# A two-layer hybrid decoder trunk: spread of the condition, first norm, and the places of the adaLN sums

## What is computed

```python
cond = silu(c)
for l in range(2):
    sh1, sc1, g1, sh2, sc2, g2 = split(cond @ w_ada[l] + b_ada[l], 6)
    h = rms_norm(x, norm1[l]) * (1 + sc1) + sh1
    x = x + g1 * token_mixer(h, ...)   # three attention branches, gated, one output projection
    h = rms_norm(x, norm2[l]) * (1 + sc2) + sh2
    x = x + g2 * swiglu(h, w_gu[l], w_down[l])
```

## Time and profile before

| | |
|---|---|
| median of 3 runs | 1011.0 us (1010.39 to 1011.73) |
| profiled execution, its own time | 1010.04 us |
| its span, first to last instruction | 1008.2 us |
| TensorE busy | 934.6 us, 93% |
| VectorE busy | 695.9 us, 69% |
| ScalarE busy | 474.8 us, 47% |
| moved by DMA | 198.83 MB, mean 197 GB/s |
| mean granted TensorE clock | 0.964 |

### The profile page before, as it was taken

The page is one execution under the profiler, slowest core; times in us unless marked ns, Lnnn a source line. Parts: engine busy times, 40 slices in busy tenths (PEclk is TensorE's granted clock), DMA queues, the critical chain, the costliest instruction groups (busy, mean ns, idle before and its releaser), DMA issues.

```text
span 1008.2 us, 15872 instructions
## 1 busy us (share of the span) xinstructions
PE 934.6 (93%) x6716; PEld 885.0 (88%) x6716; DVE 695.9 (69%) x1097; ACT 474.8 (47%) x642; POOL 24.3 (2%) x48
## 2 busy tenths in 40 slices
PE   3899989999885999999988999899999989999998
PEld 2689979877884999999987899799779889999998
DVE  2977789786885778686845367897867754656443
ACT  4344976356232443443344349754553544434341
POOL 1000000000000000000000000000000000000000
PEclk9999999999895899999987999999999989999999
DMA  9777533414575488888852474334145525665541
GB/s 375 280 288 282 178 110 118 160 47 183 216 266 207 159 302 324 301 305 318 289 217 83 141 274 162 125 126 168 43 167 176 201 89 193 217 223 174 194 167 42
DMA packets 29446, 198.83 MB, mean 197 GB/s; under 512 B 3264, under 2 KB 3648, under 8 KB 7232
## 3 DMA queue, kind: packets, MB, share of 16 engines
q1 hardware_dynamic: 23184, 154.74, 43.1%
q0 software_dynamic: 5760, 41.95, 11.0%
q10 hardware_dynamic: 432, 1.14, 0.3%
HBM read 196.76 MB, written 1.05 MB: 196 GB/s over the span
## 4 chain that ended last, share of the span: by engine, by line
PE 67%; DVE 19%; ACT 9%; issue 3%; DMA 2%; ACTq 0%; DVEq 0%
PE bank L448 17%; PE bank L450 16%; PE bank L449 16%; DVE w_lo L1084 5%; ACT w_hi L819 3%; PE bank L526 3%; PE bank L527 3%; PE bank L528 3%; PE bank L470 2%; DVE front L1091 2%; DVE score L1246 2%; PE bank L545 2%; PE bank L544 2%; PE bank L546 2%; DVE acc L1337 1%
## 5 line engine op out<-in xcount | busy, mean ns | idle before, releaser
L1084 DVE TENSOR_TENSOR w_lo<-raw,w_hi 128x2048 fp32r<-128x2048 f32 (+2 forms) x146 | 314.2, 2160 | 138.8 <-ACT w_hi L819 138.6
L448 PE MATMUL bank<-h_hi,w_hi 128*128 128x256 f32 x1216 | 351.4, 289 | 9.1 <-DVE w_lo L1084 4.8
L819 ACT ACTIVATE w_hi<-raw 128x2048 fp32r<-128x2048 f32 (+2 forms) x146 | 262.7, 1806 | 185.0 <-PE bank L450 121.3
L449 PE MATMUL bank<-h_lo,w_hi 128*128 128x256 f32 x1216 | 347.6, 286 | 0.0
L450 PE MATMUL bank<-h_hi,w_lo 128*128 128x256 f32 x1216 | 347.5, 286 | 0.0
L448 PEld LDWEIGHTS bank<-h_hi,w_hi 128*128 128x128 f32 x1216 | 237.2, 195 | 13.1 <-issue 12.2
L449 PEld LDWEIGHTS bank<-h_lo,w_hi 128*128 128x128 f32 x1216 | 237.2, 195 | 0.1
L450 PEld LDWEIGHTS bank<-h_hi,w_lo 128*128 128x128 f32 x1216 | 236.9, 195 | 0.0
L448 PE MATMUL bank<-y_hi,w_hi 128*128 128x256 f32 x480 | 138.4, 288 | 5.5 <-DVE proj L1399 4.5
L449 PE MATMUL bank<-y_lo,w_hi 128*128 128x256 f32 x480 | 137.4, 286 | 0.0
L450 PE MATMUL bank<-y_hi,w_lo 128*128 128x256 f32 x480 | 137.2, 286 | 0.0
(11 more groups left out here) (158 smaller groups left out, 1077.9 us busy)
## 6 DMA issues: line engine op xcount, KB each, us to landing
raw<-in_slabs_dram SPq DMA_DIRECT2D x124, 1024.0 KB, 5.1
front<-in_ada_dram POOLq DMA_DIRECT2D x40, 1024.0 KB, 5.8
raw<-in_slabs_dram SPq DMA_DIRECT2D x16, 552.0 KB, 4.1
front<-in_ada_dram SPq DMA_DIRECT2D x5, 1024.0 KB, 14.2
raw<-in_slabs_dram SPq DMA_DIRECT2D x6, 768.0 KB, 5.1
proj<-in_ada_dram SPq DMA_DIRECT2D x2, 1024.0 KB, 7.6
x_t<-in_x_dram SPq DMA_DIRECT2D x1, 1024.0 KB, 5.3
acc<-in_ada_dram SPq DMA_DIRECT2D x1, 1024.0 KB, 7.1
```

The costliest lines, as they stand in the source:

```text
L448: nc.tensor.matmul(b_out, st_hi, mv_hi, start=start, stop=False, skip_group_check=True)
L449: nc.tensor.matmul(b_out, st_hi, mv_lo, start=False, stop=False, skip_group_check=True)
L819: nc.scalar.activation(w_hi[:, n % RING, 0:w], raw[:, n % RING, 0:w], ACT.Copy).then_inc(hi_ready.sem, 1)
L1084: nc.vector.tensor_tensor(w_lo[:, n % RING, 0:w], raw[:, n % RING, 0:w], w_hi[:, n % RING, 0:w], ALU.subtract).then_inc(lo_ready.sem, 1)
```

## The change

- `c` comes as one row. A product with a row of ones spreads it into two PSUM banks, from which ScalarE takes Silu. x comes in two halves; of the constants only the identity comes early. VectorE squares the first half of x, ScalarE the second; squares and sums go by pairs of channel tiles.
- `busy(n)` issues n products of zeros on TensorE: 5 ahead of the sums, 3 between sums and transposes, 4 behind the transposes, in layer 0's first norm alone.
- The norm has two steps: VectorE forms x * rstd for two tiles at once (`norm_by_token`), ScalarE applies coefficient and shift (`norm_scaled`) and rounds (`norm_hi`), VectorE subtracts. It is VectorE that copies `rstd`.
- The first slab of pass A runs its products kind by kind, eight of each.
- The sums of `w_ada` stand, in each layer: 6 in pass B, 2 at the gates, 2 around w_uq, 2 in attention; then 12 in the MLP of layer 0 and 4 in that of layer 1. There are three places for tiles.
- At the layer boundary one `lo` is moved among the updates of x, and of the sums of squares one pair stands inside the last `down`.

```diff
-ADA_B = [(0, A_B + i) for i in range(4)]
-ADA_W = [(0, A_W + i) for i in range(8)]
-ADA_F = [(0, A_F + i) for i in range(4)] + [(1, A_P + i) for i in range(8)] + [(1, A_W + i) for i in range(8)]
-ADA_B1 = [(1, A_B + i) for i in range(4)]
-ADA_F1 = [(1, A_F + i) for i in range(4)]
-ADA_SEQ = ADA_B + ADA_W + ADA_F + ADA_B1 + ADA_F1
+ADA_SEQ = []
+for _l in range(DEPTH):
+    _tiles = [(_l, A_B + i) for i in range(12)]
+    ADA_SEQ += [(*_tiles[i], i % 3) for i in range(6)] + [(*_tiles[i], i % 2) for i in range(6, 12)]
+    _tiles = [(_l, A_F + i) for i in range(4)] + ([(_l + 1, A_P + i) for i in range(8)] if _l + 1 < DEPTH else [])
+    ADA_SEQ += [(*t, i % 3) for i, t in enumerate(_tiles)]
...
+        ada_raw = [front_w[:, 2048 * i:2048 * (i + 1)] for i in range(2)] + [acc[:, 0:2048]]
+        norm_sq = [proj[:, i // 2, 2048 + 2 * T * (i % 2):2048 + 2 * T * (i % 2 + 1)] for i in range(4)]
...
+        norm_h = [proj[:, 0, 2048 + T * i:2048 + T * (i + 1)] for i in range(4)]
...
-            sp.dma_start(x_t[:, :, :].rearrange("p a t -> p (a t)"), x).then_inc(x_in.sem, 16)
+            sp.dma_start(cond[0:1, :], c.unsqueeze(0)).then_inc(cond_in.sem, 16)
+            for m in range(2):
+                sp.dma_start(x_t[:, 4 * m:4 * m + 4, :].rearrange("p a t -> p (a t)"),
+                             x[:, 4 * T * m:4 * T * (m + 1)]).then_inc(x_in[m].sem, 16)
...
+            sp.dma_start(konst[:, P:], const[:, P:]).then_inc(konst_in.sem, 16)
...
+                l, tile, place = ADA_SEQ[n]
+                before = [i for i in range(n) if ADA_SEQ[i][2] == place]
+                pool.wait_ge(ada_used.sem, KT + (before[-1] + 1 if before else 0))
+                pool.dma_start(ada_raw[place], ada[l, tile]).then_inc(ada_in[place].sem, 16)
...
-                for _ in range(4):
+                for _ in range(10):
...
-                pool.wait_ge(scored.sem, scored.at(l, NH))
-                for _ in range(len(ADA_W) + len(ADA_F) if l == 0 else len(ADA_F1)):
+                pool.wait_ge(scored.sem, scored.at(l, B_HEADS + A_HEADS))
+                for _ in range(2):
                     load_ada(n)
                     n += 1
+                pool.wait_ge(pv_done.sem, pv_done.at(l, NH))
+                for _ in range(12 if l + 1 < DEPTH else 4):
+                    load_ada(n)
+                    n += 1
...
+            pe.wait_ge(cond_in.sem, 16)
+            for m in range(2):
+                last = nc.tensor.matmul(bank[m][:, :], ones_row, cond[0:1, 512 * m:512 * (m + 1)], start=True, stop=True)
+            last.then_inc(cond_row.sem, 1)
...
+            def busy(n):
+                for _ in range(n):
+                    nc.tensor.matmul(bank[2][:, 0:T], kz_t[:, 0, 0:P], kz_t[:, 0, :], start=True, stop=True)
+            pe.wait_ge(zeros_ok.sem, 2)
+            busy(5)
+            pe.wait_ge(ones_ok.sem, 2)
...
+            def norm_sum(l, which, p):
+                if l == 0 and which == 0 and p < 2:
+                    pe.wait_ge(sqv_done.sem, p + 1)
+                else:
+                    pe.wait_ge(sq_done.sem, sq_done.at(l, 4 * which + p - 1))
...
+                for kk in range(2):
+                    for t in range(TT):
...
+                if p == 3:
+                    last.then_inc(ss_done.sem, 1)
...
+                    for p in range(4):
+                        norm_sum(0, 0, p)
+                    busy(3)
+                    pe.wait_ge(ident_in.sem, 16)
                 norm_spread(l, 0)
+                if l == 0:
+                    busy(4)
...
+                    if k == 0:
+                        pe.wait_ge(hi_ready.sem, hi_ready.at(l, S_A + 1))
+                        pe.wait_ge(hhi_done.sem, hhi_done.at(l, 1))
+                        slot = (l * NS + S_A) % RING
+                        tiles = [(bank[4 * t + cc][:, :], slice(t * P, (t + 1) * P), slice(512 * cc, 512 * (cc + 1)))
+                                 for t in range(TT) for cc in range(4)]
+                        for o, at, col in tiles:
+                            nc.tensor.matmul(o, h_hi[:, 0, at], w_hi[:, slot, col], start=True, stop=False)
+                        pe.wait_ge(hlo_done.sem, hlo_done.at(l, 1))
+                        for o, at, col in tiles:
+                            nc.tensor.matmul(o, h_lo[:, 0, at], w_hi[:, slot, col], start=False, stop=False)
+                        slab(l, S_A)
+                        for o, at, col in tiles:
+                            last = nc.tensor.matmul(o, h_hi[:, 0, at], w_lo[:, slot, col], start=False, stop=False)
+                        last.then_inc(slab_used.sem, 1)
+                        continue
...
-                            if l + 1 < DEPTH and m >= 3:
-                                norm_sum(l + 1, 0, m - 3)
+                            if l + 1 < DEPTH and m == 5:
+                                norm_sum(l + 1, 0, 0)
...
-                    for k in range(4, KT):
-                        norm_sum(l + 1, 0, k)
+                    for p in range(1, 4):
+                        norm_sum(l + 1, 0, p)
...
-            nc.scalar.dma_start(cond[:], c.partition_broadcast(P)).then_inc(cond_in.sem, 16)
-            nc.scalar.dma_start(konst[:], const).then_inc(konst_in.sem, 16)
-            act.wait_ge(cond_in.sem, 16)
-            nc.scalar.activation(cond[:], cond[:], ACT.Silu).then_inc(cond_ok.sem, 1)
-            act.wait_ge(zeros_ok.sem, 3)
+            nc.scalar.dma_start(konst[:, 0:P], const[:, 0:P]).then_inc(ident_in.sem, 16)
...
+                for p in range(4):
...
+                        act.wait_ge(x_in[1].sem, 16)
+                    nc.scalar.activation(norm_sq[p], x_t[:, 2 * p:2 * p + 2, :].rearrange("p a t -> p (a t)"),
+                                         ACT.Square).then_inc(sq_done.sem, 1)
+            def norm_std(l, which):
+                act.wait_ge(ss_done.sem, ss_done.at(l, which + 1))
+                nc.scalar.activation(std_t, bank[NORM_BANKS[which][0]][:, 0:TT], ACT.Sqrt, bias=eps, scale=1.0 / D)\
+                    .then_inc(std_done.sem, 1)
...
+            def norm_scaled(l, which, k):
...
+                at = (SH2 if which else SH1) + k
+                nc.scalar.activation(norm_h[k % 4], norm_x[k % 4], ACT.Identity, bias=mod[:, l, at:at + 1],
+                                     scale=coef[:, l, 8 * which + k:8 * which + k + 1]).then_inc(hs_done.sem, 1)
+            def norm_hi(l, which, k):
+                act.wait_ge(hs_done.sem, hs_done.at(l, KT * which + k + 1))
+                nc.scalar.activation(h_hi[:, k, :], norm_h[k % 4], ACT.Copy).then_inc(hhi_done.sem, 1)
...
+                    act.wait_ge(zeros_ok.sem, 1)
+                    table(ACT.Silu)
+                    act.wait_ge(cond_row.sem, 1)
+                    for m in range(2):
+                        nc.scalar.activation(cond[:, 512 * m:512 * (m + 1)], bank[m][:, :], ACT.Silu)\
+                            .then_inc(cond_ok.sem, 1)
+                    table(ACT.Sqrt)
                     norm_squares(0, 0)
+                    norm_std(0, 0)
                     hi(0, S_A)
-                    norm_scale(0, 0)
-                    norm_hi(0, 0, 0)
-                    for k in range(1, KT):
-                        hi(0, S_A + k)
+                    for k in range(KT):
+                        act.wait_ge(coef_done.sem, k + 1)
+                        norm_scaled(0, 0, k)
                         norm_hi(0, 0, k)
+                        if k + 1 < KT:
+                            hi(0, S_A + k + 1)
                 else:
...
+                act.wait_ge(ada_used.sem, KT + (24 if l else 0) + 6)
...
+                norm_std(l, 1)
...
+            for p in range(2):
+                if p == 0:
+                    dve.wait_ge(x_in[0].sem, 16)
+                xs = x_t[:, 2 * p:2 * p + 2, :].rearrange("p a t -> p (a t)")
+                nc.vector.tensor_tensor(norm_sq[p], xs, xs, ALU.mult).then_inc(sqv_done.sem, 1)
...
+                dve.wait_ge(rs_tp.sem, rs_tp.at(l, which + 1))
+                nc.vector.tensor_copy(rstd[:], bank[NORM_BANKS[which][1]][:, 0:T]).then_inc(rstd_done.sem, 1)
+                dve.wait_ge(rstd_done.sem, rstd_done.at(l, which + 1))
...
+            def norm_by_token(l, which, p):
+                if p >= 2:
+                    dve.wait_ge(hs_done.sem, hs_done.at(l, KT * which + 2 * p - 2))
+                nc.vector.tensor_tensor(proj[:, 1, 2048 + 2 * T * (p % 2):2048 + 2 * T * (p % 2 + 1)]
+                                        .rearrange("p (a t) -> p a t", a=2), x_t[:, 2 * p:2 * p + 2, :],
+                                        rstd[:, :].unsqueeze(1).to_broadcast([P, 2, T]), ALU.mult)\
+                    .then_inc(xr_done.sem, 1)
...
-                nc.vector.scalar_tensor_tensor(out=h_lo[:, k, :], in0=norm_x[k % 4], scalar=mod[:, l, at:at + 1],
-                                               in1=h_hi[:, k, :], op0=ALU.add, op1=ALU.subtract)\
```

(27 more changed lines are left out.)

130 lines of the change are left out of this document (61 added, 69 removed).

## The result

The changed kernel takes 991.74 us (median of 4 runs, 989.68 to 997.31), the kernel before beside it 1010.69: a ratio of 0.9827, 95% interval 0.9803 to 0.9852. It is faster, by 19.0 us between the medians and by 17.5 by the ratio, where 32.3 was forecast; 978.7 lies 13.0 us too low. The time stands at the very top of the range of 970 to 992; carried over by the ratio, 0.9827 of 1011.0 is 993.5, just above it. The profiled execution took 991.47 (span 989.3, granted clock 0.976); TensorE's idle time (span less busy time) fell from 73.6 to 53.6 us.

The account below looks back on a forecast made before the run. TensorE's back-to-back matmuls were taken to bound most of the span, so only stages where it waits could pay. The terms summed to -32.3 us, 977.7 from the profiled 1010.04, carried over as 978.7; range 970 to 992.

Parts of the forecast that it names:

- Pass B and gates, layer 0: Layer 0's pass B and gates: six sums instead of three, two instead of one; charged +1 us (0 to +6).
- rival A: Transfers from release of w_ada places to the w_uq slab: VectorE waits for two tiles, +9 us, 988; 16%.
- gaps in pass B: Sign that the forecast is wrong: TensorE shows gaps in pass B; no size given.
- Prologue, the start: Layer 0's start up to the first w_in matmul: at about 15.7 us, 10.6 earlier than 26.34.
- rival B: Cold clock: zero products don't raise it or sums let it fall; prologue +5.8, boundary +2, 986 us; 14%.
- Pass A: Layer 0's pass A after the start: ends at 62 to 64 us, not 75.56; term with the start -12.5.
- Indexer: Indexer's stage, both layers: a double sum before pair_sums(1) delays the chain; +3.2 us a layer, +6.4 (+4 to +10).
- Attention: Attention, both layers: sums at steps 15 and 17, the first partly showing; +1.5 us a layer, +3 (+1 to +6).
- Branches, layer 0: Layer 0's branches and second norm: eight double sums, a transfer wait and the clock's fall leave; -23.4 us (-20 to -25).
- No gap over 1 us: Sign of being right: no such TensorE gap in layer 0's branches, and both layers' windows within 2 us.
- Norms: The norms: dearer channel tiles and a later first h_hi against waits that leave; 0 us (-1 to +2).
- Boundary: Layer boundary: one w_lo before x, one pair of sums inside; transposes near 526.2, not 533.00; -6.8 us (-9 to -3).

Follow-up runs that it names:

- the kernel with moves undone: Changed kernel with the w_ada sums and loads back at their earlier places and two tile places; prologue, norms and boundary stay changed: 998.77 us, ratio 0.9861 to 0.991.

## Why the prediction was wrong

Direction and place were right, the size was not: a measured sum of -18.6 stands against -32.3. By its own terms:

- **Pass B and gates, layer 0: +1 forecast (0 to +6), +7.0 measured. This step failed.** The step charged the work of VectorE and TensorE against each other, found them even and stopped there. That part holds (38.50 without loads). What it put at nothing was the transfers, left to rival A: a need of 376 GB/s as the mean of 42 us, set against 424 from the prologue. The mean hid the timing. The first three loads were released within 1.2 us of each other, at 58, the other five up to 85.8, and from 60 to 92 us the DMA engines were full at 392 to 426 GB/s. Each of the last six slabs of pass B then took 8.3 to 11.0 us to land, and with three places that is a slab every 3.8 us, where TensorE's work is 3.0. Rival A named the right cause (+9, 988) with the wrong wait: it had VectorE waiting for two tiles, but VectorE waited for one, 1.51 us at 63.42, and the late ones were the slabs, awaited by ScalarE. Its sign, gaps in pass B, is weak too: they were 0.52 us and less, with one of 3.23 behind pass B. The 7.0 are about 2.1 in pass B, 3.3 in that gap and 1.6 in the gate slabs, where the granted clock was 0.79 from 96 to 104 us. The Trainium skill's figure of 358 GB/s as a core's share (DMA: Bandwidth & Descriptors) does not bind here; the trace shows up to 426.
- **Prologue, the start: -10.6 forecast, -6.3 in this profile and about -3.2 in four of eleven. This step failed too.** Three sizes were wrong. The five products ahead of the sums were given to 8.5 or 10.8 and the sums an end at 12.0, which goes with 8.5; they took to 10.26, and the sums, all behind them, ended at 14.3 even at the upper level: 2.3 lost. The three products behind were charged 0.4 and cost 1.7 to 1.9, for the clock had fallen (0.74 from 12 to 14 us, 0.50 from 14 to 16): 1.3 lost. From the transposes to the first matmul the sum had 2.45 and 3.20 was measured. That the products would hurt was no rival of mine; rival B, sums at the lower level, is what four of eleven profiles show on top.
- **Pass A**: from its first matmul 46.5; forecast 46.3 to 48.3, with 47.4 in the term. Right, and 0.9 better than the term.
- **Indexer: +6.4 forecast, +6.5 measured.** The square root, 9.8 behind w_uq's start before, stands 13.0 behind it, as forecast (126.9 against 113.93). Right, by the chain told. Placing the sums elsewhere takes it off in full.
- **Attention: +3 forecast, +2.3 measured** (+1.5 and +0.8), of which the kernel with moves undone shows +1.3 and 0.0, so that in layer 0 most of it isn't the sums'. That leaves about 1.0 to the sums: right in size, in good part by luck.
- **Branches, layer 0: -23.4 forecast, -23.5 measured**, and -20.5 where the clock fell earlier (60.6). The window of layer 1 was the right control. No gap over 1 us came in the branches, as the sign had it, apart from 1.46 at the first sum of the second norm; the two windows differ by 2.84 us and not by under 2, for the reason under "Norms".
- **Boundary: -6.8 forecast, -5.8 measured.** Right.
- **Norms: 0 forecast.** Layer 1's second norm took 2.7 more. It is no price of the change that can be shown: between the end of attention and that norm the changed kernel and its variants mostly read either 57.7 to 58.2 or 60.4 to 61.1, in either layer (58.8 to 59.2 and 62.1 occur); in the changed kernel's profile layer 0 has the short one with PEclk 1.00 and layer 1 the long one with 0.94 (windows above). Before was seen once, at 57.79. Whether the change makes the longer case more frequent is open; that would take more profiles of the kernel before.

Between the profiled executions the gap is 13.7 (-18.6 against -32.3): 6.0 from pass B, 3.5 from the prologue with pass A, 2.7 from layer 1's clock, 1.0 from the boundary, less 0.7 in attention, and 1.2 in shifts of about 0.5 or less each.

## What to carry to other kernels

Where a stage lives on a short ring of buffers, ask not for the mean rate over the stage but for what else is in flight when each buffer's load is issued. Here it helped to put bulk loads into the same queue, in the order of use, and to start them where the DMA engines stood idle; the two were won together. Before warming TensorE with products, look at whether what they precede is on its critical path and what waits behind it: here the second slab waited for VectorE, and the higher clock won nothing in pass A. And place extra work by the rows in which an engine waits for something else: the two sums of the indexer's stage came in front of work that others waited for, and cost 3.2 us a layer.

## What the runs showed of the hardware

- Which level TensorE runs at differs between executions at such places: 32 rows of sums took 4.22 us or 6.83 us with the same instructions ahead of them. The Trainium skill (TensorE: Matmul & The Clock Gate, "What's actually happening") says that the number of slow matmuls at a start varies from run to run; the trace agrees, and shows it in the middle of a kernel as well.
- The granted clock prints 1.00 from 10 to 12 us in all eleven profiles. In the four in which the sums took 0.21 a row, the duration of the lower level, it goes on printing 1.00 to 20 us. There it does not tell the level; the duration of a matmul does.
- A slab of 552 KB took 3.8 us in the median of eight from issue to landing where no w_ada tile was loaded (layer 0's pass B without loads), and up to 11.0 (issued at 61.93, landed at 72.94) in the changed kernel beside w_ada tiles.
